# A decoder layer with 32 experts: the expert loop turned, whole weight matrices per load, and a second DMA queue for the down matrices

## The reference

```python
h = rmsnorm(x, mix_norm_g)
q_a, k_a, v_a, q_b, k_b, v_b, g_a, g_b = split(h @ w_in)          # w_in: 1024 x 4352
a = moba_attention(q_a, k_a, v_a); b = swa_attention(q_b, k_b, v_b, sinks)
merged = sigmoid(g_a) * (a @ moba_out_w) + sigmoid(g_b) * (b @ swa_out_w)
x = x + merged @ mix_out_w
x = x + cross_attention(rmsnorm(x, xattn_norm_g), rmsnorm(mem, mem_norm_g), ...)
x = x + hier_moe(rmsnorm(x, ffn_norm_g), ...)
return rmsnorm(x, final_norm_g)

def hier_moe(h, ...):       # 4 groups of 8 experts; top group, then two of its experts
    for g in range(4):
        hid = silu(einsum('nd,edf->nef', h, w_gate[g])) * einsum('nd,edf->nef', h, w_up[g]) * combine[:, g]
        out = out + einsum('nef,efd->nd', hid, w_down[g])         # gate, up 1024 x 256; down 256 x 1024
```

## Time and profile before

| | |
|---|---|
| median of 3 runs | 459.22 us (457.35 to 460.4) |
| profiled execution, its own time | 457.95 us |
| its span | 456.2 us |
| PE busy in the span | 404.4 us (89%) |
| DVE, ACT, POOL busy | 176.3, 167.0, 38.9 us |
| read from HBM | 138.06 MB |
| mean granted PE clock | 0.974 of full |

### The profile page before, as it was taken

One profiled execution on the slowest core, in us unless ns is written; L12 is line 12 of the kernel. 1 busy time (PEld: TensorE's weight loads), 2 busy tenths in 40 slices (PEclk: granted clock), 3 DMA queues, 4 the chain that ended last, 5 costly groups with the idle time before them and its releaser, 6 DMA issues.

```text
span 456.2 us, 7756 instructions
## 1 busy us (share of the span) xinstructions
PE 404.4 (89%) x3113; PEld 304.7 (67%) x3113; DVE 176.3 (39%) x314; ACT 167.0 (37%) x320; POOL 38.9 (9%) x80
## 2 busy tenths in 40 slices
PE   3999999999999999999999888888888828768966
PEld 3999999899999999999897434343433403313423
DVE  3564574666448956645554211111111101101113
ACT  6554565667549644475737110101020100001004
POOL 4010132422100000000400200000000000000000
PEclk9999999999999999999998999999999969959999
DMA  8757875766784777656979799999999999999992
GB/s 298 215 159 234 293 248 185 230 213 212 248 252 141 218 270 252 186 184 194 351 272 407 296 427 413 401 412 408 408 410 413 422 414 420 421 409 409 410 387 93
DMA packets 61492, 139.53 MB, mean 306 GB/s; under 512 B 6006, under 2 KB 39830, under 8 KB 57366
## 3 DMA queue, kind: packets, MB, share of 16 engines
q1 hardware_dynamic: 61456, 139.12, 83.0%
q10 hardware_dynamic: 6, 0.00, 0.0%
HBM read 138.06 MB, written 1.05 MB: 305 GB/s over the span
## 4 chain that ended last, share of the span: by engine, by line
PE 66%; SPq 16%; DMA 10%; issue 3%; DVE 3%; ACT 1%; DVEq 0%; POOLq 0%; POOL 0%; ACTq 0%
PE proj L1199 13%; PE proj L1200 13%; PE proj L1201 13%; PE proj L1452 7%; SPq L391 6%; DMA moe_pair<-in_expert_w_up_dram 6%; SPq L386 5%; DMA moe_pair<-in_expert_w_down_dram 3%; SPq L385 3%; PE score L1419 3%; PE score L1478 2%; SPq L381 2%; PE attno L1274 1%; PE probt L1199 1%; PE probt L1201 1%
## 5 line engine op out<-in xcount | busy, mean ns | idle before, releaser
L835 DVE TENSOR_TENSOR w_lo<-w_raw,w_hi 128x1024 fp32r<-128x1024 f32 x66 | 81.1, 1231 | 50.8 <-ACT w_hi L585 50.4
L1452 PE MATMUL proj<-moe_pair,moe_x 128*32 128x512 f32 x512 | 63.6, 641 | 26.6 <-DMA moe_pair<-in_expert_w_up_dram 14.6
L585 ACT ACTIVATE w_hi<-w_raw 128x1024 fp32r<-128x1024 f32 x66 | 69.8, 1058 | 34.2 <-PE proj L1201 20.4
L1199 PE MATMUL proj<-hT_hi,w_hi 128*128 128x256 f32 x232 | 68.2, 294 | 0.0
L1200 PE MATMUL proj<-hT_lo,w_hi 128*128 128x256 f32 x232 | 66.5, 287 | 0.0
L1201 PE MATMUL proj<-hT_hi,w_lo 128*128 128x256 f32 x232 | 66.4, 286 | 0.0
L1452 PEld LDWEIGHTS proj<-moe_pair,moe_x 128*32 128x32 f32 x512 | 17.0, 116 | 62.1 <-issue 52.4
L789 ACT ACTIVATE hid<-proj 128x256 f32<-128x256 f32 x8 | 3.1, 384 | 145.3 <-PE proj L1452 145.3
L1135 DVE TENSOR_TENSOR moe_x<-score,gains_moe 128x512 f32<-128x512 f32 x16 | 11.1, 692 | 99.7 <-PE score L1419 99.7
L1199 PEld LDWEIGHTS proj<-hT_hi,w_hi 128*128 128x128 f32 x232 | 45.4, 196 | 3.2 <-issue 2.3
L1200 PEld LDWEIGHTS proj<-hT_lo,w_hi 128*128 128x128 f32 x232 | 45.4, 196 | 0.0
(11 more groups left out here) (263 smaller groups left out, 741.2 us busy)
## 6 DMA issues: line engine op xcount, KB each, us to landing
moe_pair<-in_expert_w_down_dram SPq DMA_DIRECT2D x64, 512.0 KB, 15.4
w_raw<-in_w_in_dram SPq DMA_DIRECT2D x34, 512.0 KB, 4.4
moe_pair<-in_expert_w_gate_dram SPq DMA_DIRECT2D x32, 512.0 KB, 14.5
moe_pair<-in_expert_w_up_dram SPq DMA_DIRECT2D x32, 512.0 KB, 15.1
moe_pair<-in_expert_w_gate_dram SPq DMA_DIRECT2D x16, 1024.0 KB, 15.2
moe_pair<-in_expert_w_up_dram SPq DMA_DIRECT2D x16, 1024.0 KB, 17.2
w_raw<-in_xattn_wkv_dram SPq DMA_DIRECT2D x8, 512.0 KB, 4.0
w_raw<-in_mix_out_w_dram SPq DMA_DIRECT2D x8, 512.0 KB, 5.3
```

The lines of the kernel that those rows point to most:

```text
L585: act.activation(w_hi[g % NS][:], w_raw[:, g % NW], ACT.Copy).then_inc(hi_done, 1)
L835: dve.tensor_tensor(w_lo[g % NS][:], w_raw[:, g % NW], w_hi[g % NS][:].bitcast(F32), ALU.subtract)\
L1199: pe.matmul(ps, a[0], b[0], start=start, stop=False, skip_group_check=True)
L1452: op = pe.matmul(PJ[0][e * WIN:(e + 1) * WIN, :].rearrange("p (j f) -> p j f", j=2), moe_x[:, k % 4, e * WIN:(e + 1) * WIN], both_w, start ...
```

## The change

- **Start.** PE transposes raw x as it lands; the inverse roots of x are put in when the q, k and gate chunks leave PSUM, which moves these 15 copies from ACT to DVE (v stays on ACT, with a scale). A row of the roots is made by two small PE products after the third weight half. The gains are loaded by ACT, the first of them apart. The first weight halves are loaded and split in parts. PE does six products without use before x is there and four after the second tile (`WARM`).
- **Residual.** All four residual copies stand ahead of the counting products.
- **Gather.** Four pieces of two row blocks instead of two of four, with a `moe_x` copy and a semaphore count each.
- **Quads 1 to 6** have every matrix whole: gate, up and down in rows of 8 KB, one DMA of 1 MiB each. The hidden rows are taken in the order p*2 + k to match. Quads 0 and 7 keep halves; quad 7's last two slots hold the columns 0 to 511 and 512 to 1023 of four down matrices.
- **Loop.** Quads 0, 1 and 2 come before the loop, one turn of the loop is quads 3, 4, 5, 6, and quad 7 comes behind it. The loop's count is read after quad 2.
- **Queues.** SP issues gate and up, and all of quads 0, 1 and 7. ACT issues the down matrices of quads 2 to 6 (`load_down`), those of quad n between its work on quad n-1 and on quad n.

```diff
-            normalise(0, xres, [1])
...
+            part_lo(0, 0)
             dve.wait_ge(c_gain, 1)
             unit_lo(0, hT_hi, hT_lo, 0)
             unit_lo(0, hT_hi, hT_lo, 1)
+            part_lo(0, 1)
+            part_lo(1, 0)
...
+                if kinds[c] in ON_DVE:
+                    evacuate(c)
...
+            for t in range(TT):
+                pe.wait_ge(x_in[t], 16)
+                for u in range(4):
+                    op = transpose_unit(NT_BANKS, xres, u, t)
+                    if t == TT - 1:
+                        op.then_inc(nt_ps, 1)
+                warm(WARM[1 + t])
...
             copy_residual(0)
+            copy_residual(1).then_inc(res_copied, 1)
...
             def gather(half):
                 for k in range(half * 4, half * 4 + 4):
                     for t in range(TT):
-                        op = pe.matmul(SC[half][:, (k % 4) * P:(k % 4 + 1) * P], xg[:, t, k * P:(k + 1) * P],
+                        op = pe.matmul(SC[k // 2 % 2][:, (k % 2) * P:(k % 2 + 1) * P], xg[:, t, k * P:(k + 1) * P],
                                        sel[:, t].rearrange("p e s -> p (e s)"), start=t == 0, stop=t == TT - 1)
-                op.then_inc(gather_ps, 1)
+                    if k % 2 == 1:
+                        op.then_inc(gather_ps, 1)
```

SP's part in the expert quads, with `user_before(i) = i - SLOTS + 1`:

```diff
-            for i in range(SLOTS, BODY_CHUNKS):
-                sp.wait_ge(chunk_used, previous_user(i) + 1)
-                load_experts(i, 0)
+            LAST = LAST_QUAD * MOE_CHUNKS
+            for i in range(SLOTS, SLOTS + GU_CHUNKS):
+                sp.wait_ge(chunk_used, user_before(i))
+                load_whole(i, 0)
             sp.wait_ge(trips_set, 1)
...
-            with sp.Fori(1, total) as body:
-                for i in range(BODY_CHUNKS):
-                    sp.wait_ge(chunk_used, body * BODY_CHUNKS + previous_user(i) + 1)
-                    load_experts(i, body % BODIES)
...
+            with sp.Fori(0, turns) as turn:
+                for i in range(LAST, LAST + BODY_CHUNKS):
+                    if i % MOE_CHUNKS < GU_CHUNKS:
+                        sp.wait_ge(chunk_used, turn * BODY_CHUNKS + user_before(i))
+                        load_whole(i % BODY_CHUNKS, (turn + i // BODY_CHUNKS) % BODIES)
+            for c in range(MOE_CHUNKS):
+                sp.wait_ge(chunk_used, turns * BODY_CHUNKS + user_before(LAST + c))
+                load_last(c)
```

ACT's part:

```diff
+            def load_down(q, quads_used, body):
+                act.wait_ge(chunk_used, quads_used * MOE_CHUNKS)
+                for e in range(QE):
+                    s = slot_of_chunk(q * MOE_CHUNKS + GU_CHUNKS + e)
+                    act.dma_start(slots[s][:].unsqueeze(1),
+                                  whole_down_v[:, bass.ds((body * BODY_QUADS + q) * QE + e, 1), :])\
+                        .then_inc(moe_in[s], 16)
+
+            for q in range(LAST_QUAD):
+                if q == 2:
+                    load_down(2, 1, 0)
+                expert_quad(q)
...
+            with act.Fori(0, turns) as turn:
+                for q in range(LAST_QUAD, LAST_QUAD + BODY_QUADS):
+                    load_down(q % BODY_QUADS, turn * BODY_QUADS + (q - 1), (turn + q // BODY_QUADS) % BODIES)
+                    expert_quad(turn * BODY_QUADS + q)
+            expert_quad(turns * BODY_QUADS + LAST_QUAD)
```

PE's last quad (`down_columns(half)` makes the products of the second 128 hidden rows for one half of the columns):

```diff
+                down_pairs(LAST_QUAD, 0, 0)
+                pe.wait_ge(selT_sb, n + 1)
+                down_pairs(LAST_QUAD, 1, 0)
+                pe.wait_ge(last_in[GU_CHUNKS + 2], 16)
+                down_columns(0).then_inc(y0_ps, 1)
+                pe.wait_ge(y_act, n + 1)
+                back_to_tokens(0, 0)
+                pe.wait_ge(last_in[GU_CHUNKS + 3], 16)
+                down_columns(1)
+                back_to_tokens(1, 0)
+                pe.wait_ge(y_dve, n + 1)
+                for t in range(TT):
+                    back_to_tokens(t, 1)
```

More of the change, by code:

```diff
@@ L105, in hybrid_layer, with user_before @@
     SLOTS = 24
-    WIDE = (1, 2)
+    LAST_QUAD = BODY_QUADS - 1
     def slot_of_chunk(i):
         return i % SLOTS
[L112 to L118, removed]
     def landed(i, body):
[L122 to L128, removed]
+        q = i // MOE_CHUNKS
+        return body * 32 + (0, 16, 16, 32)[q]
+    def user_before(i):
+        return i - SLOTS + 1
     RUN = 4
@@ new lines, in gate_up_by_halves @@
+            def gate_up_by_halves(q, n, arrived):
+                for k in range(KD):
+                    kh, r = divmod(k, RUN)
+                    if r == 0:
+                        if kh == 1:
+                            gather(1)
+                        for e in range(QE):
+                            pe.wait_ge(arrived[kh * QE + e], 32)
+                    if k % 2 == 0:
+                        pe.wait_ge(moe_x_sb, n * 4 + k // 2 + 1)
+                    for e in range(QE):
+                        s = slot_of_chunk(q * MOE_CHUNKS + kh * QE + e)
+                        both_w = slots[s][:].rearrange("p (j r f) -> p r j f", j=2, r=RUN)[:, r]
+                        op = pe.matmul(PJ[0][e * WIN:(e + 1) * WIN, :].rearrange("p (j f) -> p j f", j=2),
+                                       moe_x[:, k % 4, e * WIN:(e + 1) * WIN], both_w,
+                                       start=k == 0, stop=k == KD - 1)
+                        if r == RUN - 1:
+                            op.then_inc(chunk_used, 1)
@@ new lines, in _, with down_product, down_pairs @@
+            hid_halves = hid[:].rearrange("p (k f) -> p k f", k=KF)
+            hid_by_rows = hid[:].rearrange("p (f k) -> p k f", k=KF)
+            def down_product(half, kt, e, weights):
+                return pe.matmul(SC[half][e * WIN:(e + 1) * WIN, :], hidT[:, kt, e * WIN:(e + 1) * WIN], weights,
+                                 start=kt == 0, stop=kt == KF - 1)
+            def down_pairs(q, half, kt):
+                for e in range(QE):
+                    s = slot_of_chunk(q * MOE_CHUNKS + GU_CHUNKS + 2 * kt + e // 2)
+                    col = (e % 2) * D + half * 512
+                    op = down_product(half, kt, e, slots[s][:, col:col + 512])
+                    if half == 1 and e % 2 == 1:
+                        op.then_inc(chunk_used, 1)
+                return op
@@ new lines, in back_to_tokens, with results @@
+            def back_to_tokens(t, half):
+                pe.matmul(ACC[t][half][:], selwT[:, t * P:(t + 1) * P], (y0_sb, y1_sb)[half][:], start=False,
+                          stop=True, skip_group_check=True).then_inc(back_ps[t][half], 1)
+            def results(n):
+                pe.wait_ge(y_act, n + 1)
+                back_to_tokens(0, 0)
+                back_to_tokens(1, 0)
+                pe.wait_ge(y_dve, n + 1)
+                for t in range(TT):
+                    back_to_tokens(t, 1)
+                pe.wait_ge(sel_made, n * 2 + 3)
+                gather(0)
```

511 lines of the change are left out of this document (303 added, 208 removed).

## The result

The changed kernel takes 467.13 us (median of 4 runs, 466.6 to 467.59); the kernel before, run beside it, 459.06 (457.35 to 460.4). The ratio is 1.0177, 95% interval 1.0142 to 1.0213: slower by 8 us. The profiled execution took 467.21 us, its span is 465.5.

A forecast was written before the change was run, and what follows sets the result against it. It took PE to bound the first part and the expert-weight byte stream the second; -3.2 - 2.7 + 0.5 + 7.0 - 1.8 = -0.2 us gave 459.0 us against the median of 459.22, range 454 to 469.

The forecast's parts named there:

- the second queue: Quads 2 to 6: ACT's down-load chain, 25.6 to 28.2 us, stays hidden under the stream's 29.8 us a quad; no price.
- the sum: Whole kernel: start, stream, row, hole and end terms add up to -0.2 us, 459.0 against the median of 459.22.
- Rival A: Quads 2 to 6: ACT's down-load chain decides instead of the stream; 462 to 467 us, middle 464; chance 0.22.
- The hole: Expert weight stream stands still once, before quad 2's late-issued down matrices: +7.0 us, between 5.5 and 8.
- The stream: Expert weights: whole rows run at 422 instead of 410 GB/s, -2.7 us; also +0.5 for 2 KB rows and +7.0 standstill.
- rival D: Expert weights: 409 and 422 GB/s come from the moment, not row size; sum +2.5, 461.7 us; little chance.
- Rival B: ACT's down loads wait behind SP's queued loads, then alternate; +15 us after slack, 474 us; chance 0.13.
- C: Faster: start gives 4.0, hole is 5.5, two queues feed engines 1% better; 453 to 455 us; chance 0.18.
- The start: First products: raw x transposed on landing, scaling moved into evacuations; gain 2.4 to 4.0 us, taken as -3.2.
- the hand-over into the experts: Router to first expert products: residual copies delay the gather 1.3 us, the finer gather pays it back; net 0.
- The end: Behind the last load: 3.7 us of products and copies instead of 5.5, -1.8 us if PE is waiting for it.
- The 0.5 for rows of 2 KB: Last 2 MiB of weights: rows of 2 KB run slower than 4 KB ones, between 0 and +0.5 us, taken as +0.5.

The follow-up runs named there:

- e4: Changed kernel with 30 (quad 6: 14) products without use ahead of PE's waits for down matrices in quads 2 to 6; 457.85 us.
- e10: Changed kernel with quad 2's down matrices issued one quad earlier and products without use ahead of the down waits in quads 3 to 6; 450.48 us.
- e1: Changed kernel with ACT issuing all its down loads one quad earlier, ahead of its work on the quad before; 457.17 us.
- e5: Changed kernel with only the down loads of quads 3 to 6 issued one quad earlier, quad 2's left late; 461.68 us.
- e3: Changed kernel with only quad 2's down load issued one quad earlier, those of quads 3 to 6 left late; 457.92 us.
- e8: e2 with each whole matrix of quads 1 to 6 loaded by two DMAs with rows of 4 KB; 457.85 us.
- e2: Changed kernel with all down loads on SP's queue in chunk order, still whole matrices, none issued by ACT; 451.50 us.
- e9: e2 with the last quad's down matrices as before: whole pairs in rows of 4 KB, last products in the old order; 451.71 us.
- e6: The kernel before with the change's new start alone and no other part; 455.92 us.
- e7: Changed kernel with ACT's down issues moved from behind the y copy of the quad before to behind its hidT copy; 461.39 us.
- e11: e2 with products without use ahead of PE's gate and up waits in quads 4 to 6 and two waits in quad 7; 452.58 us.

## Why the prediction was wrong

**The step that failed is "the second queue".** It compared ACT's chain in one quad, 25.6 us, 28.2 with PE at its lower clock, with the stream's 29.8 and called it hidden. So it added nothing to the sum. The link measures 30.7, and the chain is what PE waits for. Term by term, forecast and measured: to the first byte 1.6, 3.3; 4 MiB at half rate 19.9, 19.8; to the wait's end 0.6, 2.5; products 2.85, 4.87; y copy and issue 0.65, 0.2. The share was right. I took the first byte's 1.6 from an issue of SP into a nearly idle stream (in the changed kernel SP's issue at 278.74, behind the hole, has its first packets 1.0 us later). Here SP's loads keep every DMA engine busy, and the links of quads 3 to 6 have 3.3 to 3.5. Whether the full stream or ACT's queue makes the difference no run tells. For the 0.6 to the wait's end there was no row; the 14 straggling packets and the release took 2.5. And the clock's 2.0 us a link I had seen in the earlier trace rows (6.19 us after a wait of 8) and put in the second place, though the waits that the chain makes are of just that length. Rival A had the right mechanism and, with 28.2 a link, a middle of 464; its link was 2.5 us short. The measured time lies at A's upper end; that it is also inside my whole range is no merit of the sum, which said no change.

**The clock is why it tips over.** At full clock two of these e4 links measure 28.3 or 28.4 and one 29.6 (y copies at 312.19, 341.76, 370.12, 398.44), under 29.8, and the time is near the forecast: 457.85 against 459.0, with a first part 2.4 us better than its term, so that the nearness is in part luck. At the lower level (0.50 in the window from 428 to 432, that is 1.2 GHz) the first four links are 30.6 to 31.3, over 29.8. Then PE falls behind the stream by a little in each quad, waits for ACT's load, and is slow because it has waited: its clock is down at 0.50 in 305 to 309 already, while it still waits, and through the products behind. Over the five links the changed kernel's y copies fall 11 us behind e4's (433.23 against 422.26 in quad 6), and its span is 11.3 longer. From PE's release to the y copy the five links take 4.8 to 5.4 us in place of e4's 2.84, which is 11.3 in all: the clock accounts for the whole difference of the two traces.

**The hole** was right: predicted 7.0 (5.5 to 8); the window from 274.5 to 280 has a DMA share of 0.13, and the rate falls at 274.0 and is back near 280.5, 6.5 us. In time it is worth 7.4 us where the chain is at full clock (e10 against e4, which differ in it and in quad 2's filler), and 4.5 where the down loads go early and PE waits for gate and up (e1 against e5). e3, which has none, is 9.2 us faster than the changed kernel, with one link less. It is not visible in the sum of the changed kernel alone, as the chain starts from the same late issue.

**The stream.** 422 GB/s with rows of 8 KB and 410 to 413 behind them, as taken from the earlier trace rows; e8 and the last 2 MiB of e2 and e9 show that it goes with the rows' size (rival D is out). The Trainium skill's rule (DMA: Bandwidth & Descriptors, "Queues, rings and completion order"), that the DMA engines take turns between queues, agrees: 557 packets to 559. It agrees again, and more sharply, where the packets differ in size: while SP loads quad 7 in rows of 4 KB (411 to 425) both queues have 527 packets, and ACT's moves 3.92 MB, SP's 1.90. Rival B, behind the backlog, is out by the same row. So is the hope of C that two queues feed the engines better: 421 with one, 420 with two. The first part came 5.6 us earlier, more than C's 4.0 for the start, but the chain took it.

**The start** itself was sized about right in the trace: e6 has 3.5 us at the first quad, forecast 3.2. My working for it was not: the loads listed for ACT and DVE add up to 10.2 us, which from 6.2 gives 16.4 and not the 15.3 written; measured, the third half begins at 14.95, 5.2 earlier than before, and the small products then take 1.3 of that and not 0.8. At the first quad the sum was 2.4 short (-3.2 against -5.6), because I put the hand-over into the experts at net 0; there the copies, moved ahead, fall into a wait of PE for the router, and the finer gather gives its 0.8. In time, e6 shows less than I gave.

**The end**, -1.8 + 0.5, was put at a place where PE waits for the last byte. In the changed kernel it doesn't. In e2 it does, and e9 shows no gain there either: the eight last products run 1.66 us at the lower clock level after short waits, the sixteen old ones 1.92 at the full one. From the last down products to the end of the span e2 takes 11.7 us, as before (from 444.51), e9 12.1; e4 and e10, whose PE is at full clock there, take 10.0 and 10.1. So the 1.8 is there, but only at full clock. The 0.5 for rows of 2 KB was near: 2.1 MB at 386 instead of 410 GB/s are 0.3.

What decides now: in the changed kernel ACT's chain; in e2 the stream, at its 421 GB/s. In e10 the last products stand at 438.30, as in e2, with PE at work right up to them, so stream and PE end together.

## What to carry to other kernels

A load on a second queue that is issued behind its consumer's work is a chain: issue, first byte, its bytes at half the rate, the stragglers, the consumer, the engine that issues again. Add it up for the loaded stream, with the consumer at the clock that it has after such a wait, and ask for a margin of several microseconds against the stream's period, since a chain just over the period makes waits that make it longer. Two queues that share by turns take rate from the load that is needed first when the other goes early (e1, e7); one queue in order of need was as fast as the best kernel with two (e2, e10). And where an engine in such a chain waits long, useless work in the wait can be worth more than any saving, while e11 shows no gain from it where the stream decides (9.3 us in e4).

## What the runs showed of the hardware

- Two queues with 8 KB rows share evenly by packets (557 to 559 in 19.5 us), and the sum is that of one (420 to 422 GB/s). With packets of two sizes the numbers stay equal (527 to 527 in 411 to 425) and the bytes don't: 3.92 MB for the queue with rows of 8 KB, 1.90 for the one with 4 KB.
- Into a full stream the second queue's first packets came 3.3 us after the issue (3.3 to 3.5 in four links), and PE was released 2.5 us after the bulk was through, with 14 packets of that queue in between.
- After a wait of 9.5 us PE made 32 product records in 5.61 us (clock 0.50 in 335 to 343), after 7 us of filler and a wait of 2.35 in 3.64.
- Rows of 8 KB ran at 421 GB/s (e2), rows of 4 KB at 409 (e8, with DMAs of half the size), rows of 2 KB at 386 (e2, 430 to 434, DMAs of 1 MiB).
